# Two key projections of a cross-attention rewritten as seven half-size block products each

## The reference

```
h = x + W_out [ RWKV7_group(P) || DiffAttn_group(P) ],  P = RMSNorm(x) @ W_in
memn = RMSNorm(mem)
kv = memn @ wkv                       # (256, 1024) @ (1024, 2048)
km, vm = split(kv, 2)                 # keys and values, 4 heads of 256
h = h + softmax(q km^T / 16) vm @ wo  # q = RMSNorm(h) @ wq
h = h + MoE(RMSNorm(h))               # top 4 of 32 experts, 12.6 MB of weights each
out = RMSNorm(h)
```

## Time and profile before

| | |
|---|---|
| median of 3 executions | 1218.3 us (1218.21 to 1219.0) |
| the profiled execution | 1220.18 us, its span 1218.5 us |
| PE busy | 1184.0 us, 97% of the span |
| DVE, ACT busy | 330.0 us, 195.2 us |
| moved by DMA | 445.46 MB, mean 366 GB/s |
| granted TensorE clock, mean | 1.00 |

### The profile page before, as it was taken

One profiled execution on the slowest core, in us unless ns is written; L12 is line 12 of the kernel. 1 busy time (PEld: TensorE's weight loads), 2 busy tenths in 40 slices (PEclk: granted clock), 3 DMA queues, 4 the chain that ended last, 5 costly groups with the idle time before them and its releaser, 6 DMA issues.

```text
span 1218.5 us, 17685 instructions
## 1 busy us (share of the span) xinstructions
PE 1184.0 (97%) x7480; PEld 563.7 (46%) x7480; DVE 330.0 (27%) x793; ACT 195.2 (16%) x374; POOL 14.7 (1%) x58
## 2 busy tenths in 40 slices
PE   8999999999999999999999999999999999999998
PEld 7887878888533333333333333333333333333334
DVE  4784268231421112111221112111211111111212
ACT  1322242121211111111111111111111111111102
POOL 4000000000000000000000000000000000000000
PEclk9999999999999999999999999999999999999999
DMA  9543217639899999999999999999999999999995
GB/s 332 213 128 101 106 42 306 276 121 394 335 404 421 420 433 431 436 434 430 430 430 431 431 432 431 431 432 435 434 430 431 430 430 432 432 430 431 428 428 239
DMA packets 33086, 445.46 MB, mean 366 GB/s; under 512 B 8784, under 2 KB 9168, under 8 KB 11920
## 3 DMA queue, kind: packets, MB, share of 16 engines
q1 hardware_dynamic: 28112, 443.75, 86.7%
q10 hardware_dynamic: 4928, 1.05, 0.4%
HBM read 443.47 MB, written 1.31 MB: 365 GB/s over the span
## 4 chain that ended last, share of the span: by engine, by line
PE 89%; DMA 4%; DVE 2%; ACT 2%; another core or an unknown queue 1%; issue 1%; DVEq 0%; SPq 0%; ACTq 0%
PE ps L1647 35%; PE ps L1689 17%; PE ps L1058 9%; PE ps L1079 5%; PE ps L1609 5%; PE ps L1591 5%; DMA arena<-in_moe_w 4%; PE ps L1575 3%; PE ps L1422 2%; PE ps L1597 2%; ACT arena L1004 1%; PE ps L1602 1%; PE ps L1093 1%; PE ps L1119 1%
## 5 line engine op out<-in xcount | busy, mean ns | idle before, releaser
L1647 PE MATMUL ps<-ring,arena 128*64 128x512 f32 x1056 | 230.6, 593 | 7.4 <-DMA ring<-in_moe_w 6.6
L1647 PE MATMUL ps<-arena 128*64 128x512 f32 x984 | 215.0, 593 | 7.6 <-DMA arena<-in_moe_w 7.6
L1647 PEld LDWEIGHTS ps<-ring,arena 128*64 128x64 f32 x1056 | 75.5, 137 | 159.2 <-issue 149.0
L1647 PEld LDWEIGHTS ps<-arena 128*64 128x64 f32 x984 | 70.2, 137 | 149.6 <-issue 137.6
L996 ACT ACTIVATE arena<-ps 128x512 f32<-128x512 f32 x31 | 18.5, 597 | 670.7 <-DVE ps L2353 670.7
L2353 DVE TENSOR_SCALAR ps<-ps 128x512 f32<-128x512 f32 x31 | 21.7, 699 | 382.0 <-PE ps L1647 382.0
L1689 PE MATMUL ps<-arena 128*64 128x512 f32 x512 | 113.6, 595 | 0.5 <-DMA arena<-in_moe_w 0.5
L1689 PE MATMUL ps<-ring,arena 128*64 128x512 f32 x480 | 106.3, 595 | 0.0
L1058 PE MATMUL ps<-arena,ring 128*128 128x256 f32 x448 | 98.9, 380 | 0.3 <-DVE arena L1885 0.3
L1058 PEld LDWEIGHTS ps<-arena,ring 128*128 128x128 f32 x448 | 84.5, 190 | 12.8 <-issue 1.4
L2366 DVE COPY arena<-ps 128x512 f32<-128x512 f32 x31 | 21.4, 691 | 225.3 <-PE ps L1689 225.3
(11 more groups left out here) (327 smaller groups left out, 896.0 us busy)
## 6 DMA issues: line engine op xcount, KB each, us to landing
ring<-in_moe_w SPq DMA_DIRECT2D x39, 4096.0 KB, 36.3
arena<-in_moe_w SPq DMA_DIRECT2D x36, 4096.0 KB, 41.0
arena<-in_moe_w SPq DMA_DIRECT2D x15, 2048.0 KB, 15.3
ring<-in_moe_w SPq DMA_DIRECT2D x10, 2048.0 KB, 44.0
arena<-in_moe_w SPq DMA_DIRECT2D x17, 1024.0 KB, 10.4
ring<-in_moe_w SPq DMA_DIRECT2D x14, 1024.0 KB, 8.1
ring<-in_w_in SPq DMA_DIRECT2D x12, 1024.0 KB, 5.0
ring<-in_wkv_x SPq DMA_DIRECT2D x8, 1024.0 KB, 4.8
```

The costliest lines, as they stand in the source:

```text
L1647: ins = t.matmul(ps[c * BLK:(c + 1) * BLK, 4 + b, :], xeT[:, col:col + BLK], w(k % 4)[:, f0:f0 + 512], start=False, stop=(k == KC - 1), sk ...
```

## The change

kv0 and kv1 are each computed as a two by two block product. The 1024 rows of the weights are cut into two halves (k blocks 0..3 and 4..7), the 256 columns of a chunk into left and right, the 256 memory tokens into two halves. Seven products of half-size blocks, each with four matmuls of 128 x 128 against 128 tokens, take the place of eight. Four sums of memory blocks (t1 to t4, once) and four sums of weight blocks for each chunk (s1 to s4) are made by VectorE; each is 128 x 512. The products of the two chunks go into banks 0 and 1 in turns, four at each place where half a chunk stood and two at the last; three of a chunk's seven are added to what lies in their bank. Of each chunk's results ScalarE copies three blocks of 128 x 128 and VectorE moves four, one as a copy, three as sums with what is in `kmT`. The sums t1 to t4 and s1, s3, s2 of kv0 stand on VectorE between `combine(0)` and the sum of VX; s1, s3, s2 of kv1 between that sum and `score_max(1)`. SP's list is unchanged, but the chunks kv3 and kv4 now wait for the last of the seven products of kv0 and kv1.

```diff
@@ banks
-        chunk("kv0")
...
-        chunk("kv1")
+        KEY_STEPS = [(m, step) for m in range(2) for step in ("x11w11", "x12w21", "s2t2", "s3t3", "s1t1", "x22t4", "s4w22")]
+        for n, (m, step) in enumerate(KEY_STEPS):
+            place(f"keys{m}_{step}", n % 2)
+        for m in range(2):
+            where[f"kv{m}"] = where[f"keys{m}_s4w22"]
@@ ScalarE
-            copy(kmT[:, 0:2, :], "kv0", two)
-            for i in range(NT):
-                copy(Y0[:, i, :], f"yz{i}")
-            copy(kmT[:, 2:4, :], "kv1", two)
+            def key_block(m, step, q, i):
+                copy(kmT[:, 2 * m + q, i * P:(i + 1) * P], f"keys{m}_{step}", lambda v: v[:, 0:P])
+
+            key_block(0, "x11w11", 0, 0)
+            key_block(0, "s2t2", 1, 0)
+            key_block(0, "s4w22", 0, 1)
+            key_block(1, "x11w11", 0, 0)
+            copy(Y0[:, 0, :], "yz0")
+            key_block(1, "s2t2", 1, 0)
+            copy(Y0[:, 1, :], "yz1")
+            key_block(1, "s4w22", 0, 1)
@@ TensorE
-            key_parts = itertools.chain(turned_parts("kv0", memT), turned_parts("kv1", memT))
-            next(key_parts)
-            next(key_parts)
+            def key_product(m, step):
+
+                o = begin(pe, f"keys{m}_{step}")
+                w = weights(f"kv{m}")
+                s1, s2 = key_sums[m]
+                t1, t2, t3, t4 = key_columns
+                lo, hi, left, right = slice(0, NP), slice(NP, KC), slice(0, P), slice(P, WCOL)
+                lhs, rhs, needs = {"x11w11": (w[:, lo, left], memT[:, lo, 0:P], None), "x12w21": (w[:, hi, left], memT[:, hi, 0:P], None),
+                                   "s2t2": (s2, t2, f"s2_{m}"), "s3t3": (w[:, lo, right], t3, f"s3_{m}"), "s1t1": (s1, t1, f"s1_{m}"),
+                                   "x22t4": (w[:, hi, right], t4, "t4"), "s4w22": (w[:, hi, left], memT[:, hi, P:T], f"s4_{m}")}[step]
+                if needs is not None:
+                    pe.wait_ge(sem("operands_ready"), 1 + OPERANDS.index("k_" + needs))
+                opens = step in ("x11w11", "x12w21", "s3t3")
+                for k in range(NP):
+                    ins = t.matmul(o[:, 0:P], lhs[:, k, :], rhs[:, k, :], start=(opens and k == 0), stop=(k == NP - 1), skip_group_check=True)
+                done(ins, f"keys{m}_{step}")
+
+            for m, step in KEY_STEPS[0:4]:
+                key_product(m, step)
@@ TensorE, between Rh, yz0 and yz1, and behind yz1
-                next(key_parts)
-                next(key_parts)
+                for m, step in KEY_STEPS[4 + 4 * i:8 + 4 * i]:
+                    key_product(m, step)
...
-            for _ in key_parts:
-                pass
+            for m, step in KEY_STEPS[12:]:
+                key_product(m, step)
@@ VectorE
+            def key_block(m, step):
+
+                q, i, other = {"x12w21": (0, 0, "x11w11"), "s3t3": (1, 1, None), "s1t1": (1, 1, None), "x22t4": (1, 0, "s2t2")}[step]
+                dst = kmT[:, 2 * m + q, i * P:(i + 1) * P]
+                if other:
+                    taken(dve, f"keys{m}_{other}")
+                o = product(dve, f"keys{m}_{step}")[:, 0:P]
+                if step == "s3t3":
+                    dlink(v.tensor_copy(dst, o), f"keys{m}_{step}")
+                else:
+                    dlink(v.tensor_tensor(dst, o, dst, ALU.add), f"keys{m}_{step}")
...
+            for nm in ("s1", "s3", "s2"):
+                key_sum(nm, 0)
             flat4 = lambda x: x.rearrange("p i h k -> p (i h k)")
             o = product(dve, "VX")
             dlink(v.tensor_tensor(flat4(XfT), o, flat4(XTb), ALU.add), "VX")
             dve.sem_inc(sem("inverse_ready"), 1)
+            for nm in ("s1", "s3", "s2"):
+                key_sum(nm, 1)
             score_max(1)
...
                 drain(v.tensor_copy(Zf[:, i, h0:h0 + 4, :], o), f"z3{q}")
+            key_block(0, "x12w21")
+            key_sum("s4", 0)
+            key_block(0, "s3t3")
...
                 drain(v.tensor_tensor(tok, o, AR[:, :, :, 1, c * CH:(c + 1) * CH], ALU.add), f"Rh{c}")
+            for step in ("s1t1", "x22t4"):
+                key_block(0, step)
             combine(1)
+            key_block(1, "x12w21")
+            key_sum("s4", 1)
+            for step in ("s3t3", "s1t1", "x22t4"):
+                key_block(1, step)
             score_max(2)
```

More of the change, by code:

```diff
@@ L469, in program @@
                       for m in range(2)]
-        OPERANDS = ["s3", "t3_0", "s1", "t3_1", "s2", "s4", "t1_0", "t2_0", "t1_1", "t2_1", "t4_0", "t4_1"]
+        OPERANDS = ["k_t3", "k_t1", "k_t2", "k_t4", "k_s1_0", "k_s3_0", "k_s2_0", "k_s1_1", "k_s3_1", "k_s2_1", "k_s4_0", "k_s4_1",
+                    "s3", "t3_0", "s1", "t3_1", "s2", "s4", "t1_0", "t2_0", "t1_1", "t2_1", "t4_0", "t4_1"]
+        key_names = [name for name in OPERANDS if name.startswith("k_")]
+        key_columns = [ring[:, 7, 512 * n:512 * (n + 1)].rearrange("p (k t) -> p k t", k=NP) for n in range(4)]
+        key_sums = [[ring[:, 6, 512 * n:512 * (n + 1)].rearrange("p (k t) -> p k t", k=NP) for n in (2 * m, 2 * m + 1)] for m in range(2)]
         place_landed = [sem(f"place{p}_landed") for p in range(2 * SLOTS)]
@@ L1451, in _ @@
                     taken(pe, f"kv{c}")
+                    if c < 2:
+                        taken(pe, f"keys{c}_x22t4")
                 for i in range(NT):
@@ L2063, in _, with key_operand, key_sum @@
             combine(0)
+            key_made = [0]
+            def key_operand(name, dst, in0, in1, op):
+                assert OPERANDS[key_made[0]] == "k_" + name
+                key_made[0] += 1
+                v.tensor_tensor(dst, in0, in1, op).then_inc(sem("operands_ready"), 1)
+                dve.wait_ge(sem("operands_ready"), key_made[0])
+            def key_sum(name, m):
+                w = home(ORDER.index(f"kv{m}")).rearrange("p (k n) -> p k n", k=KC)
+                s1, s2 = key_sums[m]
+                lo_, hi_, left, right = slice(0, NP), slice(NP, KC), slice(0, P), slice(P, WCOL)
+                if name == "s1":
+                    chunk_landed(dve, f"kv{m}")
+                dst, in0, in1, op = {"s1": (s1, w[:, lo_, right], w[:, hi_, right], ALU.add),
+                                     "s3": (w[:, lo_, right], w[:, lo_, left], w[:, lo_, right], ALU.subtract),
+                                     "s2": (s2, s1, w[:, lo_, left], ALU.subtract),
+                                     "s4": (w[:, hi_, left], w[:, hi_, left], s2, ALU.subtract)}[name]
+                key_operand(f"{name}_{m}", dst, in0, in1, op)
+            def key_block(m, step):
[8 more added lines that the diff above has]
+                    dlink(v.tensor_tensor(dst, o, dst, ALU.add), f"keys{m}_{step}")
+            c1, c2, c3, c4 = key_columns
+            for nm, dst, in0, in1 in (("t3", c3, memT[:, NP:KC, P:T], memT[:, 0:NP, P:T]), ("t1", c1, memT[:, 0:NP, P:T], memT[:, 0:NP, 0:P]),
+                                      ("t2", c2, memT[:, NP:KC, P:T], c1), ("t4", c4, memT[:, NP:KC, 0:P], c2)):
+                key_operand(nm, dst, in0, in1, ALU.subtract)
+            for nm in ("s1", "s3", "s2"):
+                key_sum(nm, 0)
             flat4 = lambda x: x.rearrange("p i h k -> p (i h k)")
@@ L2158, in operand @@
                 dve.wait_ge(sem("operands_ready"), operands[0])
-            operands = [0]
+            operands = [len(key_names)]
             def right(name, m):
```

## The result

The changed kernel takes 1223.92 us, the median of 6 executions (1222.5 to 1225.1), against 1218.89 us for the kernel before (6 executions, 1218.21 to 1220.24). The ratio is 1.0037, with a 95% interval of 1.0027 to 1.0047: slower by about 5.0 us by the medians (4.5 by the ratio), where +0.8 was forecast and the range ended at 1220.4.

What follows compares the result with a forecast made beforehand. TensorE's chain in the mixers was taken to start the expert transfers that set the end; -1.3 + 0.1 + 0 + 2.0 = +0.8 us on a median of 1218.3 gave 1219.1 us, range 1216.6 to 1220.4.

Steps and rivals of the forecast that it cites:

- Where the time is bounded: In the mixers TensorE's own chain binds; it starts the expert transfers, so a microsecond there is worth about one at the end.
- the first filler of kv2: Sign on TensorE's timeline behind the mixers' products: it starts at 159.7 us, before at 158.90.
- R4: Rival at the end of the kernel: the change doesn't reach it, 1218.3 us; chance 0.10.
- Term 1: Products of kv0 and kv1 on TensorE: seven smaller ones take 13.2 us in place of 14.5, -1.3 us.
- Term 2: Two banks used in turns for the products: moving blocks out is hidden unless the moving engine is busy, +0.1 us.
- R3: Rival at the new products: the banks bind, each waits for the last but one's moving out, 1220.9 us; chance 0.08.
- Term 3: New sums on VectorE around the sum of VX fit into its holes: 0, covered by 1.0 us at the closest place.
- Term 4: Instruction fetch held behind kv4's transfer: 3.6 us gap at `values(0)`, then 0.2, for the old 1.03 and 0.75; +2.0 us.
- R1: Rival at the fetch near kv4's transfer: it is not held up, gaps about as before, 1217.1 us; chance 0.22.
- R2: Rival at TensorE's instruction fetches: no gap is left, 1215.3 us; chance 0.05.
- The clock: TensorE's granted clock in the mixers: 1.00 in every window, the 2.4 GHz level, and no change counted from it.
- slower: Outcome of the whole kernel: R3 just exceeding 2.4 us, or a fetch that waits still longer; together 0.07.

Runs made afterwards that it cites:

- run 1: The kernel before with 109 already satisfied waits added in TensorE's idle time of the first 100 us, moving its instruction block edges; 1224.99 us, ratio 1.0043.
- run 3: The changed kernel with SyncE issuing the load of kv4 later, only when group S1 is filled; 1220.20 us, ratio 1.0006.
- run 4: The kernel before with SyncE issuing the load of kv4 later, only when group S1 is filled; 1218.22 us, ratio 0.9987.
- run 8: The kernel before with the later load of kv4 and ScalarE copying at0 nine times instead of once, so TensorE waits; 1224.07 us, ratio 1.0035.
- run 9: The changed kernel with the later load of kv4 and 24 satisfied waits in TensorE's idle time of the first 100 us; 1221.26 us, ratio 1.0010.
- run 10: The changed kernel with the later load of kv4 and 40 satisfied waits in TensorE's idle time of the first 100 us; 1220.51 us, ratio 1.0006.
- run 12: The changed kernel with the last two products of kv1 moved behind `states(0)` and the later load of kv4; 1219.90 us, ratio 1.0004.
- run 7: The changed kernel, kv4 loaded as it was, with 184 satisfied waits in TensorE's idle time of the first 100 us; 1225.39 us, ratio 1.0047.
- run 5: The changed kernel with the later load of kv4 and 184 satisfied waits in TensorE's idle time of the first 100 us; 1225.11 us, ratio 1.0039.
- run 6: The kernel before with the later load of kv4 and 184 satisfied waits in TensorE's idle time of the first 100 us; 1224.07 us, ratio 1.0031.
- run 2: The changed kernel with 147 satisfied waits in TensorE's idle time of the first 100 us, meant to restore the old block edges; 1228.1 us, ratio 1.0067.
- run 11: The changed kernel with the last two products of kv1 moved behind `states(0)`, kv4 loaded as it was; 1223.72 us, ratio 1.0033.

## Why the prediction was wrong

**Where the time is bounded** was right: the first filler of kv2 came 3.74 us late, and 3.1 us of it reached the end. R4 (nothing reaches the end) is out.

**Term 1, products, -1.3.** Right: by the chain 13.30 us for 14.60, so -1.3. (The last group is 1.98 there and 1.89 from start to start, as the forecast counted.)

**Term 2, banks, +0.1, and R3.** A block takes 0.28 or 0.29 us to move out, and no idle time of TensorE beside the products is put down to VectorE or ScalarE. The price is 0, and R3 is out; run 1, with the old products in the old banks, loses the same 5 us.

**Term 3, sums on VectorE, 0.** Right: the seven end at 118.72 (118.7 forecast), with 0.80 us to spare.

**Term 4, fetches, +2.0.** The mechanism was right in place and size: 3.80 us at the start of `values(0)` for 3.6 forecast, with the packet behind kv4's transfer, and both older gaps of the earlier trace rows gone. R1 and R2, which had no gap of that size, are out. Not foreseen were 0.67 us in yz0, which is one edge earlier, and 0.11 in yz1: the prediction worked out the edges of the two gaps and not of every block behind the keys, though the 1.17 us at 117.92 was a third gap in its own trace.

**The clock: the step that failed.** The text read 1.00 in every window of before and said: "PE will be no less busy; I count no change from it". Its fourth term forecast that PE would stand still for 3.6 us. A gap of that length does not cost its length alone. From the row at 154.30 to the one at 162.64 the same work takes 8.3 us; at full clock it is 0.94 + 1.06 + 0.59 + 1.73 + 1.09 + 0.63 = 6.0 us by the chains of runs 1, 3 and 4 and its own rows. That is +2.3 us. Run 8 shows that idle time alone does this. The Trainium skill, page "TensorE: Matmul & The Clock Gate", section "Why this matters for your kernels", says to leave no long idle gaps of TensorE between bursts of matmuls, or it goes back to the half rate; by that rule the forecast gap should have carried this price. The trace (3.80 us) and run 8 (3.66) agree with it. The runs show falls behind much shorter idle times as well (0.83 us in run 3), where the measurement decides.

The sum by traces: -1.3 + 0 + 0 + (3.80 + 0.67 + 0.11 - 1.03 - 0.75 = 2.8) + 2.3 = +3.8. From the first product of kv0 the filler came 3.95 us later than before, and 3.74 on the time axis of the trace, since kv0 began 0.21 earlier. Two terms were left out of +0.8: the clock (2.3) and the gaps in yz0 and yz1 (0.8). The spans are 3.1 apart; where the other 0.7 went isn't known. The 5.0 of the medians is 1.9 more: 1.3 because before's profiled execution lay above its median, 0.6 because that of after lay below. A difference forecast from one trace onto medians carries that much.

**The range** (its upper end adds up to 1220.2 by its own terms, not 1220.4) was too narrow because no case in it had the gap as forecast and a second cost behind it; the chance of "slower" was 0.07 because R3 was the only way there that had a price.

**What the win of the products was worth.** Run 4 against runs 3, 9, 10 and 12 says that even without the collision the changed kernel is 1.8 to 2.6 us behind the kernel before with the same later kv4 (runs 3 and 4 in one session, the others each against its own before). Two things add to this. With the old order no gap is left behind 119 us, where each of the four layouts of the changed kernel has 1.8 us or more. And in runs 3 and 10 the clock fell once more at the first expert, which in run 3 cost 1.70 us, as much as it had lost against run 4 by then. The first fits this reading: in this stretch the fetch of blocks is nearly the limit, and the time that the products gave up was cover for it. It is argued from five layouts, not shown; a layout of the changed kernel without gaps wasn't found, and may exist.

**What stays open:** what, beside its length, decides whether the clock falls behind an idle time (runs 3, 7, 9 and 10, and the same wait of 0.83 us at the first expert); why waits move the edges by half their number; and what, beside the clock, the slower executions of runs 5 to 7 do more than the profiled ones.

The best version of the study is run 4, the kernel before with kv4 loaded later: 1218.22 us, ratio 0.9987 (0.9978 to 0.9996), so about 1.4 us faster than before, where the changed kernel is 5.0 slower. It is within the 0.2% named in the prediction, though its interval is below 1.

## What to carry to other kernels

When a forecast contains a stall of TensorE of a few microseconds, add the half clock behind it: here 2.3 us for a gap of 3.8. Behind stalls of 0.8 to 1.8 us give it a chance: here it came behind some and not behind others, for 1.6 to 1.7 us where it was priced. When a change alters the number of instructions, look at where every block of 256 ends afterwards, which work runs over each fetch, and which large transfer is then underway; the cheap cure is to issue the transfer at another time. Shortening work in a stretch of many small matmuls bought nothing here; that the shortened work had hidden a fetch is the likely reason, not a shown one.

## What the runs showed of the hardware

- TensorE's granted clock fell to 0.50 behind a wait of 3.66 us for ScalarE (run 8), behind fetch gaps of 3.80 (after), 1.40 (run 2), 1.76 (run 7) and 1.78 (runs 9 and 10), and behind a wait of 0.83 us for VectorE (run 3). It stayed at 1.00 behind gaps of 1.83 (run 3), 1.78 (run 7) and 1.45 (run 1), and behind the same wait for VectorE in before and run 4. A low stretch lasted 3.5 us (runs 2, 3, 7, 9, 10 and 11) or 6.9 to 7.0 (after, runs 1, 2 and 8).
- 109 waits that are already satisfied, in a program of over 15,000 records, cost 5.4 us. They cost nothing where they stand (the mixers' products begin at 102.62 us against 103.12 before); they moved the ends of the instruction blocks (run 1), by about half an instruction each (28 records for 109 waits, 36 for 147, 5 for 24, 9 for 40).
- A fetch of 16 KB falling due within a transfer of 1 MB was served behind it: gaps of 3.80 us (after), 4.61 (run 2) and 2.54 (run 11); without the transfer, the gap at the same instruction was 1.83 (run 3). A packet that went within the first us of the transfer was not held (run 7).
